# Projection stage of a two-layer decoder step: rotations in halves between normalised tiles, weight splits four tiles ahead

## The reference, cut to what matters

```python
def rms_norm(x, g):
    xf = x.astype(jnp.float32)
    y = xf * lax.rsqrt(jnp.mean(xf * xf, axis=-1, keepdims=True) + NORM_EPS)
    return (y * g.astype(jnp.float32)).astype(x.dtype)

def rope(x, pos):
    half = ROT_DIM // 2
...
    xf = x.astype(jnp.float32)
    x1 = xf[..., :half]
    x2 = xf[..., half:ROT_DIM]
    out = jnp.concatenate([x1 * cos - x2 * sin, x2 * cos + x1 * sin, xf[..., ROT_DIM:]], axis=-1)
    return out.astype(x.dtype)

def project_layer(x, pos, norm_g, w_in):
...
    q_a = rope(pr['q_a'].reshape(b, t, N_DIL * A_HEADS, HEAD_DIM), pos)
...
```

## Time and profile before

| what | us |
|---|---|
| median of 3 runs (1032.58 to 1035.12) | 1035.1 |
| the profiled execution | 1032.55 |
| its span in the trace | 1030.9 |
| PE busy in the span | 959.9 |
| DVE, ACT, POOL busy in the span | 597.8, 424.6, 185.7 |
| projection stage of layer 0, first matmul to the first turn of values | 112.7 |
| the same, layer 1 | 103.8 |

### The profile page before, as it was taken

One profiled execution on the slowest core, in us unless ns is written; L12 is line 12 of the kernel. 1 busy time (PEld: TensorE's weight loads), 2 busy tenths in 40 slices (PEclk: granted clock), 3 DMA queues, 4 the chain that ended last, 5 costly groups with the idle time before them and its releaser, 6 DMA issues. The chain is left out here.

```text
span 1030.9 us, 20994 instructions
## 1 busy us (share of the span) xinstructions
PE 959.9 (93%) x7852; PEld 870.9 (84%) x7852; DVE 597.8 (58%) x1309; ACT 424.6 (41%) x845; POOL 185.7 (18%) x320
## 2 busy tenths in 40 slices
PE   4999799997999999999999979999989999999996
PEld 4999697896877679999999968888877776999996
DVE  5876566566332357746777765666561324576564
ACT  5343454545222144343453335455442214443443
POOL 3000000034635530000000000002363475000000
PEclk9999899999999999999999989999999999999998
DMA  9553875446466992442645456546357698633521
GB/s 343 200 203 134 331 284 220 181 157 199 146 202 228 265 321 86 174 195 83 255 181 210 188 235 233 204 183 242 119 181 230 203 274 256 278 123 123 200 87 47
DMA packets 65478, 206.30 MB, mean 200 GB/s; under 512 B 12113, under 2 KB 49681, under 8 KB 56033
## 3 DMA queue, kind: packets, MB, share of 16 engines
q1 hardware_dynamic: 56480, 185.31, 48.8%
q0 software_dynamic: 8752, 19.63, 6.1%
q10 hardware_dynamic: 144, 0.01, 0.0%
HBM read 200.12 MB, written 40.18 MB: 233 GB/s over the span
## 5 line engine op out<-in xcount | busy, mean ns | idle before, releaser
L1639 DVE TENSOR_TENSOR big_r<-big,paged_r 128x1024 fp32r<-128x1024 f32 x160 | 194.7, 1223 | 142.5 <-ACT paged_r L1422 141.6
L964 PE MATMUL bank<-xnT_high_r,paged_r 128*128 128x288 f32 x768 | 231.6, 302 | 1.3 <-ACT kT L1482 1.3
L964 PE MATMUL bank<-xnT_r,paged_r 128*128 128x288 f32 x704 | 207.6, 295 | 0.0
L964 PE MATMUL bank<-xnT_high_r,big_r 128*128 128x288 f32 x704 | 207.1, 294 | 0.0
L964 PE MATMUL bank<-short_r,big_r 128*128 128x288 f32 x576 | 172.7, 300 | 0.0
L1422 ACT ACTIVATE paged_r<-big 128x1024 fp32r<-128x1024 f32 x160 | 166.3, 1050 | 5.8 <-DMA big<-in_w_tok 5.7
L964 PE MATMUL bank<-short_r,paged_r 128*128 128x288 f32 x448 | 138.1, 308 | 27.5 <-ACT oT_c L1390 11.9
L964 PEld LDWEIGHTS bank<-xnT_high_r,paged_r 128*128 128x128 f32 x768 | 144.0, 188 | 8.5 <-issue 4.6
L964 PE MATMUL bank<-kvp_r,paged_r 128*128 128x288 f32 x448 | 135.6, 303 | 0.0
L964 PEld LDWEIGHTS bank<-xnT_high_r,big_r 128*128 128x128 f32 x704 | 132.5, 188 | 0.0
L964 PEld LDWEIGHTS bank<-xnT_r,paged_r 128*128 128x128 f32 x704 | 132.3, 188 | 0.0
(11 more groups left out here) (317 smaller groups left out, 1468.0 us busy)
## 6 DMA issues: line engine op xcount, KB each, us to landing
big<-in_w_tok SPq DMA_DIRECT2D x13, 2048.0 KB, 8.7
big<-in_w_feat SPq DMA_DIRECT2D x12, 2048.0 KB, 8.5
big<-in_w_gate SPq DMA_DIRECT2D x10, 2048.0 KB, 8.7
out_kept_dil<-in_cache_dil SPq DMA_DIRECT2D x16, 1020.0 KB, 12.6
paged<-in_pool SPq DMA_DIRECT2D x218, 64.0 KB, 2.9
big<-in_w_up SPq DMA_DIRECT2D x12, 1024.0 KB, 8.8
paged<-in_pool POOLq DMA_DIRECT2D x166, 64.0 KB, 3.0
big<-in_kv_win SPq DMA_DIRECT2D x4, 2048.0 KB, 9.3
```

Source lines behind the costliest of these rows:

```text
L964: last = mm(out, l, r, start=(c == 0 and i == 0), stop=(c == n - 1 and i == 2))
L1639: v.tensor_tensor(l_part, full, h_part.bitcast(FP32), ALU.subtract).then_inc(*split_done.inc(s))
```

## The change

It reorders the first stage. The rotation of a group is cut into two halves of two tiles (the fifth key stays alone), put at tiles 4, 5, 7 and then every second tile from 9 to 23 (`ROPE_AT`). The eight normalised chunks stand at the even tiles from 10 to 24 (`NORM_AT`); their rounding on ACT is a step of its own (`nround`), a tile later, and `nlow` two tiles later. Rounding and splitting of a tile stand together, four tiles ahead from tile 3 on. In layer 0 the squares move ahead of the later quarters of `tok` 0, and `root` moves from tile 2 to tile 3. At the start SP waits for the first input piece and not for the second, loads `tok` 1 ahead of the five small tensors, and POOL waits for `tok` 1.

```diff
-RAW_AFTER = {("q", 2, 0): ("k", 0), ("q", 3, 0): ("q", 0), ("v", "d1"): ("q", 1), ("v", "slc"): ("k", 1)}
-
-ROPES = {TILES.index(("k", "win")): ("k", 0), K_SLC: ("k", 1)} | \
-        {TILES.index(("q", t, REP - 1)): ("q", t) for t in range(4)}
+RAW_AFTER = {("q", 2, 0): ("k", 0, 1), ("q", 3, 0): ("q", 0, 1), ("v", "d1"): ("q", 1, 1), ("v", "slc"): ("k", 1, 0)}
+
+ROPE_AT = {4: ("k", 0, 0), 5: ("k", 1, 0), 7: ("k", 0, 1)} | {9 + 4 * t + 2 * h: ("q", t, h) for t in range(4) for h in range(2)}
+NORM_AT = {10 + 2 * i: i for i in range(KT)}
...
-        if i < 12:
-            if i + 3 < 14:
-                out.append(of_tile("round", i + 3))
-            out.append(of_tile("split", i + 2))
-        if layer == 0 and i < 2:
-            out += [("square", 4 * i + z) for z in range(4)]
-        root = 0 if layer else 2
...
-        out += [("nlow", z) for z in range(KT) if z == i - 20] + [("norm", z) for z in range(KT) if z == i - 19]
...
+        if i == 0:
+            out += [of_tile("split", 2), of_tile("round", 3)]
+            if layer == 0:
+                out += [("square", 3), of_tile("split", 3)] + [("square", z) for z in range(4, KT)]
+            else:
+                out += [of_tile("split", 3), ("root",), ("rots",)]
+        elif i < 4:
+            out += tile_splits(*({1: (4,), 2: (5, 6), 3: (7,)}, {1: (4, 5), 2: (6,), 3: (7,)})[layer][i])
         elif i + 4 < len(TILES) + 2:
             out += tile_splits(i + 4)
-        if i in ROPES:
-            out.append(("rope",) + ROPES[i])
+        if (layer, i) == (0, 3):
+            out += [("root",), ("rots",)]
+        if i == (2 if layer else 5):
+            out.append(("rnt",))
+        for kind, z in (("nround", i - 1), ("nlow", i - 2), ("norm", i)):
+            if z in NORM_AT:
+                out.append((kind, NORM_AT[z]))
+        if i in ROPE_AT:
+            out.append(("rope",) + ROPE_AT[i])
...
-            sp.wait_ge(x_in[1], 16)
+            sp.wait_ge(x_in[0], 16)
...
-            pool.wait_ge(first_in[3], 16)
+            pool.wait_ge(*BIG.is_full(("tok", 1), 0))
...
-                elif k == "norm":
-                    act.wait_ge(*normed.at(s))
+                elif k == "nround":
+                    act.wait_ge(*normed.at(("norm", s[1])))
...
-                    kind, t = s[1:]
+                    kind, t, half = s[1:]
+                    part = slice(2 * half, 2 * half + (1 if (kind, t) == ("k", 1) else 2))
...
-                    source = raw_q[t][:, :, :] if kind == "q" else raw_k[t]
+                    source = raw_q[t][:, part, :] if kind == "q" else raw_k[t][:, part, :]
...
```

More of the change, by code:

```diff
@@ L360, in program_steps @@
     starts = [start(0, i) for i in range(KT)]
-    out = sum(starts[0:4], []) + halves(0, 0) + sum(starts[4:], []) + halves(0, 1)
-    out.append((0, ("round", ("tok", 0), 2)))
+    out = sum(starts[0:4], []) + halves(0, 0) + sum(starts[4:], []) + [(0, ("square", 0))] + halves(0, 1)
+    out += [(0, ("square", 1)), (0, ("square", 2)), (0, ("round", ("tok", 0), 2))]
     for layer in range(DEPTH):
@@ L662, in trunk_program @@
     normed = sig("normed", of("norm"))
-    norm_rounded = sig("norm_rounded", of("norm"))
+    norm_rounded = sig("norm_rounded", of("nround"))
     xn_split = sig("xn_split", range(KT))
@@ L855, in _ @@
                         sp.wait_ge(*big_used(*user))
[L856 to L863, removed]
+                    if (layer, key) == (0, ("tok", 0)):
+                        continue
+                    if key == ("tok", 1 if layer == 0 else 0):
+                        layer_loads = [(w_gc[:, :, :], a["w_gc"][layer]), (conv_w[:, :, :], a["conv_w"][layer]),
+                                       (ustart[:, :, :, :], a["conv_state"][layer]), (w2[:, :, :], a["w2"][layer]),
+                                       (pe_c[:, :, :], a["cmp_pe"][layer])]
                     buf, kind = bigb(key), key[0]
@@ L881, in _ @@
                     sp.dma_start(dst, src).then_inc(*ring_of(key).fill(key))
+                    if kind == "tok":
+                        while layer_loads:
+                            sp.dma_start(*layer_loads.pop(0)).then_inc(layer_in.sem, 16)
                     if key == ("feat", 5):
@@ L913, in _ @@
                 k = s[0]
[L914 to L915 removed]
+                if s == ("rope", "k", 0, 1):
+                    pool.wait_ge(*roped.at(("k", 0, 1)))
                     n_stores += store(o["keys_prompt"][layer], kT[:, :, :], stored)
@@ L1625, in _ @@
                     i = s[1]
-                    dve.wait_ge(*norm_rounded.at(("norm", i)))
+                    dve.wait_ge(*norm_rounded.at(("nround", i)))
                     v.tensor_tensor(xnT_low[:, i, :], xnT[:, i, :], xnT_high[:, i, :].bitcast(FP32), ALU.subtract)\
@@ L1648, in _ @@
                 elif k == "rope":
-                    kind, t = s[1:]
-                    i = next(j for j in ROPES if ROPES[j] == (kind, t))
-                    for j in {max(i - 1, 0), i}:
+                    kind, t, half = s[1:]
+                    part = slice(2 * half, 2 * half + (1 if (kind, t) == ("k", 1) else 2))
+                    i = {"k": 4 * t, "q": TILES.index(("q", t, 0)) if kind == "q" else 0}[kind] + part.stop - 1
+                    for j in (i - 1, i):
                         dve.wait_ge(*PJ.is_used(("proj", j)))
@@ L1666, in _ @@
                             new, new_turned = (z[rows, :, SEQ:T].rearrange("p r (b t) -> p b r t", b=REQ)
-                                               for z in (part, turned))
+                                               for z in (plain, turned))
                             out = qblk[rows, t, :, :].rearrange("p h (b k r t) -> p (h b) k r t", b=RB, k=KV, r=REP)
-                            last = v.tensor_tensor(out[:, :, kv, :, :], new, new_turned, ALU.add)
+                            last = v.tensor_tensor(out[:, :, kv, part, :], new, new_turned, ALU.add)
                     last.then_inc(*roped.inc(s[1:]))
```

24 lines of the change are left out of this document (8 added, 16 removed).

## The result

| what | before | after |
|---|---|---|
| median of 4 runs, us | 1035.11 (1032.58 to 1036.38) | 1001.56 (999.99 to 1003.76) |
| the profiled execution, us | 1032.55 | 999.99 |
| its span, us | 1030.9 | 998.3 |
| projection stage of layer 0, us | 112.74 | 92.57 |
| from there to the stage of layer 1, us | 398.75 | 398.70 |

The ratio is 0.968, 95% interval 0.9653 to 0.9707: 33.5 us between the medians, 32.6 between the spans. The four stretches add up to the span with the start of the first matmul, so the table says where the time came from: 20.17 in layer 0, 13.11 in layer 1, and the rest moved up as it was: 0.05 less between the stages, 0.82 more behind them. The forecast was 1002.

A forecast was written before the change was run, and what follows sets the result against it. PE was taken as the bound, with gain in its stops and half clock: 34.0 us less 0.1, 1.5, 0.3 and 1.0 is 31.1, from 1032.55 to 1001.5, said as 1002; range 996 to 1012.

The forecast's parts named there:

- 34.0 recoverable: Projection stages: PE's stops, half clock after them and smaller split waits lose 20.6 us in layer 0, 13.4 in layer 1.
- Squares ahead: Layer 0 start: sum of squares at about 19.7, `root` asks at 22.96, the 5.28 us stop goes; tile 1's copy costs 0.1.
- `tok` 1 sooner: Layer 0 start: earlier load of `tok` 1 is worth nothing by itself once the squares have moved.
- The compression tiles: DVE's bank copies behind half rotations make PE wait: 1.5 us in layer 0, 0.3 in layer 1.
- Rotations in halves: DVE: a half rotation takes 3.4 us, adding 4.2 us of DVE time per layer, all beside PE.
- The lead: Tiles 11 to 24: DVE needs 6.6 per pair against PE's 6.40; a lead of 5.6 covers about 1.4 of drift.
- DVE becomes the bound: Rival: half rotations of 4.0 or more exhaust the lead; at 4.5, 3.5 us per layer, about 1009; chance 0.10.
- `feat` 0: Layer 0, near tile 27: the load issued at 88.0 lands 9.7 later, costing 1.0 us.
- The slower rival: ACT waits at every `nround`, PE stops every second tile and its clock falls; needs a half of 6.3; chance 0.02.
- The sum: Whole kernel: 34.0 less 0.1, 1.5, 0.3 and 1.0 gives 31.1 us gained, 1001.5, said as 1002.
- One sign of being wrong: Stages behind the projection stages taking longer than they did would show the prediction wrong.

The follow-up runs named there:

- the norms alone: Kernel before with only the eight norms at even tiles 10 to 24 and their rounding a tile later, rotations whole: 1014.22 us, ratio 0.980.
- the squares back: Changed kernel with the squares again behind the first rounding of `tok` 1, loads and `root` still changed: ratio 0.9705, layer 0 stage 93.19 us.
- the loads back: Changed kernel with the start's transfers in their old order and waits: ratio 0.9677, layer 0 stage 93.75 us.
- The longer halves: Changed kernel with the sum of each query half rotation made again, once (1005.43 us) or three times (1027.54 us).
- the three extra sums: Changed kernel with the sum of each query half rotation made again three times, a half taking 5.58: 1027.54 us, ratio 0.9931.
- both edits of the start back: Changed kernel with squares and transfers of the start as before, `root` still behind tile 3: ratio 0.9738, layer 0 stage 97.08 us.
- a lead of three: Changed kernel with rounding and split three tiles ahead in place of four, rotations in halves: 1000.2 us, ratio 0.9678.

## Why the prediction was right, step by step

**Where the time was.** 34.0 recoverable, of which 33.3 came. The experiments split layer 0's 20.17 into 10.85 for the spread norms with their later rounding (put into the kernel before), 7.65 for the start (all three of its parts taken out of the changed kernel), and 1.7 as a remainder for halves and the earlier lead, close to the 2.0 of "issue" stops with the norms alone. In layer 1 it is 10.2 and a remainder of 2.9. The prediction named both long stops rightly and gave no price to each; it told of halves at most length, and they are the smallest part. Ahead of it the order is told too briefly: from tile 14 on the kernel before split four tiles ahead as well, as the diff shows, so the change lengthens the lead only up to there.

**Squares ahead.** Walked to a sum at 19.7 and a `root` at 22.96; they are at 19.93 and 23.21. The copy of tile 1 cost nothing.

**`tok` 1 sooner, "worth nothing by itself once the squares have moved".** Nearly: undone alone it cost about 1.0 in the stage, no difference in the ratio. It is the other half of a pair, since with the squares back the sooner load keeps the loss at about 1.0, and without it the loss is 4.5. The trace of the kernel with the loads back has the small wait that the prediction put elsewhere: 0.6 of PE for a `cmp` copy.

**The compression tiles, 1.8 us, mis-sized: nothing.** The copies came at 32.97 and 36.30 where I had 33.3 and 36.9. PE wanted the banks at 33.7 and 36.9 (100.90 less 21 and 20 tiles of 3.20), and the copies ended at 33.42 and 36.75. The half of two keys took 3.03 (32.97 - 29.94, from the split before), not 3.2, and PE came to the first of the two banks 0.5 later than walked. `tok` 2 held nobody up: ACT's waits for `tok` blocks are 1.7 us in two, both before 11 us.

**Rotations in halves.** 3.4 on the straight line, 3.40 measured. Every instruction shows why the line holds: two shuffles of half the size take 1.62 where one takes 1.48, two multiplications 1.52 against 1.36, two sums 1.38 against 1.22. So, if the rest grows with the elements, 0.14 to 0.16 of each is fixed. The Trainium skill's page "VectorE: DVE Perf Modes", section "The TRN2 errata — SBUF-src ops pay a fixed extra latency per instruction", from which the prediction estimated 0.16, agrees with these rows. That page's advice to minimise operations is right on DVE's time, by the 5.5 us above, and moves nothing on PE.

**The lead.** The drift is 0.08 per pair, not 0.2 (a pair of 6.49, not 6.6). The lead was mis-sized: not 5.6 but about 4. The 5.6 was for a split; ACT's list runs out sooner. At 57.90 ACT starts a `nround`, and the copy behind it must end by 62.5, when PE wants that bank (100.90 less 12 tiles of 3.20): 62.5 - 0.39 - 0.35 - 57.90 leaves 3.9. The longer halves measured 4.1 and 4.2. The rival "DVE becomes the bound" was told with the right mechanism. At its half of 4.5 (a pair of 7.6) it would cost 8 x 1.2 - 4.1 = 5.5 per layer by this lead, where I had 3.5 from seven pairs and a lead of 5.6.

**`feat` 0, 1.0 us, mis-sized: nothing.** Issued at 87.71 (88.0 foretold), but landed by 95.85, 8.1 later and not 9.7. The copy that frees tile 25's bank ended at 97.2, and tile 27 began at 97.7: 0.5 to spare.

**The slower rival** would have needed a half of 6.3; by the measured lead a loss of 16.3 per layer needs (16.3 + 4.1) / 8 = 2.55 per pair, a half of about 5.9, which is a whole rotation's time. The half of 5.58 came to within 0.7% of before.

**The sum.** 31.1, plus the 2.9 of waits that didn't come, less 0.7 of the 34.0 that stayed and 0.8 behind the stages, is 32.5; the profile says 32.56. The terms off by a factor were all small ones. Errors of 2.9 one way and 1.5 the other cancelled in part, so that the forecast's 1002 lies within 0.5 of the median is partly luck. One sign of being wrong that the prediction named did come: the stretch behind the second stage took 0.8 longer. It took 406.5 to 411.5 over all these kernels, with edits that don't touch it, so 0.8 tells nothing of the walk.

## What to carry to other kernels

When an in-order engine has to wait for another's result, ask for that result a step later: with the rounding in the step of its `norm`, ACT and DVE took turns and lost three quarters of what the two stages had gained. Two remedies for one wait (a shorter block, a longer lead) don't add up, so undo each alone before crediting it. A lead is measured by lengthening the work that it covers, in two sizes; it ends at the queue that runs out first, which need not be the one whose slack was reckoned.

## What the runs showed of the hardware that was not expected

**Stops of one length, with and without a fall of the clock.** From 68 us on PE stopped 1.65 to 1.67 us at every second tile with the rounding in its `norm`'s step, and the granted clock stayed at 1.00 from 40 to 120 us; in the 5.14 us stop (21.45 to 26.59) it fell, and it was 0.50 from 24 to 30. Between the two lie stops of 2.0 us in the kernel with the three extra sums. The first, which ended at 72.58, left the clock at 1.00; after the one that ended at 81.25 it was 0.56 and 0.59 from 82 to 86, and after the one that ended at 98.56 it was 0.50 from 100 to 102. So the length of a stop alone doesn't decide. The slower rival had counted on a fall after each such stop. A shorter one was followed by a fall as well: with both edits of the start back, stops of 1.71 and 0.37 us left PE busy for 1.92 of the 4 us from 24 to 28, and the clock was 0.62 from 28 to 30.

**The same stop, falls of different length.** No edit touches the stages behind, and still they did not keep their length: over all these kernels the stretch between the two projection stages took 397.06 to 401.40 us and the one behind the second 406.54 to 411.45, where the changed kernel has 398.70 and 408.02. The longest stretch between them is that of the kernel with the squares back, whose edits end before 30 us. PE's timeline of the changed kernel and of that one shows the same stop, 2 us later in the second, since all of it runs 2 us later there:

```profile
237.34 0.66 PE L977 MATMUL bank<-ident,short 128*128 128x128 f32 x4 [2.71 <-ACT PT L1500]
```

```profile
239.30 1.11 PE L979 MATMUL bank<-ident,short 128*128 128x128 f32 x4 [2.70 <-ACT PT L1502]
```

In the 10 us up to it PE's busy time agrees within 0.04 us in every microsecond. The stretches behind it, again 2 us apart (columns as above):

```profile
240.00:242.00 2.00, 2.00 (x10) 1.25 (x10) 0.66 (x2) 0.00 (x0) 2.00 (x3) 0.62 0.00 0
242.00:244.00 2.00, 2.00 (x17) 2.00 (x16) 1.56 (x10) 0.30 (x2) 0.55 (x1) 1.00 0.00 0
```

```profile
242.00:244.00 2.00, 2.00 (x12) 1.19 (x8) 0.69 (x1) 0.00 (x0) 2.00 (x3) 0.50 0.00 0
244.00:246.00 2.00, 2.00 (x11) 1.74 (x10) 1.47 (x8) 0.00 (x0) 0.51 (x1) 0.62 0.00 0
```

PE is busy in all four. By stretches of 1 us the clock was under 1.00 in four of them in the first kernel and in eight in the second, after the same work and the same stop. What decides it is not shown. Executions of one kernel differ too: the four with a lead of three spanned 996.5 to 1002.7 us, at a mean granted clock from 0.996 down to 0.990. It is a reason to judge an edit of a few us by the stage that it touches, with the rest of the span beside it.
